# First expert weights: one load moved, one split moved to other engines, one wait dropped

## The reference, cut to what matters

```python
grp_prob = jax.nn.softmax(xr @ w_group + b_group, axis=-1)
p_grp, g_sel = lax.top_k(grp_prob, 1)
exp_logits = jnp.einsum('td,dge->tge', xr, w_router) + b_router
...
w_top, e_top = lax.top_k(jax.nn.softmax(exp_logits, axis=-1), TOP_K)
...
def expert_block(args):
    xb, e = args
    hid = jax.nn.silu(xb @ w_gate[e]) * (xb @ w_up[e])
    return hid @ w_down[e]
```

## Time and profile before

| | |
|---|---|
| median of 3 runs | 1344.77 us (1341.58 to 1347.65) |
| profiled execution | 1344.94 us, of which the span from first to last instruction is 1343.1 us |
| mean granted TensorE clock | 0.988 of full |
| busy | TensorE 96%, VectorE 67%, ScalarE 54%, GpSimd 13% |
| DMA | 273.56 MB, mean 204 GB/s; 367 to 394 GB/s in most of the experts' stage |

### The profile page before, as it was taken

How to read it: one execution, slowest core, us unless ns; L and a number is a source line. 1 busy time by engine, 2 the same in 40 slices (tenths; PEclk the granted TensorE clock), 3 DMA queues, 4 the chain that set the end, 5 groups by cost and what they waited for, 6 DMA issues and landing times. The chain is left out here.

```text
span 1343.1 us, 19059 instructions
## 1 busy us (share of the span) xinstructions
PE 1292.4 (96%) x7544; PEld 1131.8 (84%) x7544; DVE 904.8 (67%) x1060; ACT 721.5 (54%) x919; POOL 179.4 (13%) x144
## 2 busy tenths in 40 slices
PE   6999999999999999989998999999999999999997
PEld 5989998999899999967887788888888888888874
DVE  6753556355645464534237889889898989888967
ACT  6351235123512351424223778888787887887844
POOL 0020112011201120430001111111111111111100
PEclk9999999999999999999996999999999999999999
DMA  7100010000000000305514999999999999999978
GB/s 206 48 16 19 30 32 32 17 32 32 32 17 32 32 32 1 126 0 225 199 63 165 369 373 377 390 390 390 393 394 386 387 384 367 382 393 375 381 284 343
DMA packets 38047, 273.56 MB, mean 204 GB/s; under 512 B 8147, under 2 KB 8403, under 8 KB 25700
## 3 DMA queue, kind: packets, MB, share of 16 engines
q1 hardware_dynamic: 28340, 251.67, 49.4%
q0 software_dynamic: 9216, 16.80, 3.3%
q10 hardware_dynamic: 432, 4.27, 0.8%
HBM read 260.11 MB, written 29.36 MB: 216 GB/s over the span
## 5 line engine op out<-in xcount | busy, mean ns | idle before, releaser
L950 DVE TENSOR_TENSOR w_lo<-w_raw,w_hi 128x2048 fp32r<-128x2048 f32 x192 | 433.0, 2286 | 33.2 <-ACT w_hi L731 32.6
L731 ACT ACTIVATE w_hi<-w_raw 128x2048 fp32r<-128x2048 f32 x192 | 360.6, 1915 | 90.6 <-DMA w_raw<-in_w_up 59.2
L1285 PE MATMUL bank<-xn_hi,p_hi 128*128 128x364 f32 (+1 forms) x672 | 229.2, 341 | 2.1 <-DVE p_lo L1736 2.1
L1287 PE MATMUL bank<-xn_hi,p_lo 128*128 128x364 f32 (+1 forms) x672 | 216.8, 323 | 0.0
L1286 PE MATMUL bank<-xn_lo,p_hi 128*128 128x364 f32 (+1 forms) x672 | 216.6, 322 | 0.0
L585 PE MATMUL bank<-w_hi,xgT_hi 128*128 128x512 f32 x512 | 206.2, 403 | 2.9 <-DVE xgT_lo L1008 2.9
L587 PE MATMUL bank<-w_hi,xgT_lo 128*128 128x512 f32 x512 | 201.2, 393 | 0.0
L586 PE MATMUL bank<-w_lo,xgT_hi 128*128 128x512 f32 x512 | 200.6, 392 | 0.0
L1285 PEld LDWEIGHTS bank<-xn_hi,p_hi 128*128 128x128 f32 x672 | 127.8, 190 | 2.9 <-DVE p_lo L1736 2.5
L1286 PEld LDWEIGHTS bank<-xn_lo,p_hi 128*128 128x128 f32 x672 | 128.0, 190 | 0.3
L1287 PEld LDWEIGHTS bank<-xn_hi,p_lo 128*128 128x128 f32 x672 | 127.6, 190 | 0.0
(11 more groups left out here) (253 smaller groups left out, 2023.1 us busy)
## 6 DMA issues: line engine op xcount, KB each, us to landing
w_raw<-in_w_down SPq DMA_DIRECT2D x32, 2048.0 KB, 10.4
w_raw<-in_w_gate SPq DMA_DIRECT2D x31, 2048.0 KB, 11.0
w_raw<-in_w_up SPq DMA_DIRECT2D x31, 2048.0 KB, 10.0
p_raw<-in_w_tiles SPq DMA_DIRECT2D x28, 512.0 KB, 3.3
arena<-y_rows SPq DMA_DIRECT2D x8, 1024.0 KB, 14.1
arena<-in_tokens SPq DMA_DIRECT2D x10, 416.0 KB
w_out_raw<-in_w_out SPq DMA_DIRECT2D x4, 1024.0 KB, 8.8
arena<-in_tokens SPq DMA_DIRECT2D x8, 512.0 KB, 4.4
```

Of the source, the lines that this page charges most:

```text
L731: nc.scalar.activation(w_hi[m][:, half], wraw[m][:, half], ACT.Copy).then_inc(hi_done[m], 1)
L950: nc.vector.tensor_tensor(w_lo[m][:, half], wraw[m][:, half], w_hi[m][:, half].bitcast(F32), ALU.subtract).then_inc(lo_done[m], 1)
L1285: nc.tensor.matmul(out[:, 0:n], p_hi[slot][:, k, :], hi, start=(k == 0), stop=False)
L1287: m = nc.tensor.matmul(out[:, 0:n], p_lo[slot][:, k, :], hi, start=False, stop=(k == KD - 1))
```

## The change

Four edits.

1. The routing's scratch tensors move off slot 2's raw buffer: `slot1h`, `ids`, `wparts` and the weights to where `w_out_hi` lay, the rest to just behind the raw buffer.
2. With that buffer free after the last `y_low`, SyncE issues the first down load in the output stage at t = 5, right behind the store of that step's h rows; it waits for `y_hi` and `y_lo` of all tiles. It goes from its old place.
3. ScalarE splits the first gate matrix right after its last norm of the output stage, once the output products are done, ahead of the routing's exponentials. The low part moves from VectorE to GpSimd: two subtractions of 128x2048 between GpSimd's memsets and its first gather.
4. SyncE no longer waits for the first gather ahead of the second gate load; it waits for hi and lo of the first gate matrix alone.

```diff
+        zt = Zone(NF - KD * L, NF)
+        slot1h = place("slot1h", zt.at, 2 * NT, 128)
...
+        zr = Zone(zy.end - 8320 + WU, zy.end - 8320 + 7680)
...
                 sp.dma_start(h_dram[rows, :], h_sb[t % 3]).then_inc(h_stored, 16)
+                if t == 5:
+                    sp.wait_ge(y_hi_done, 5)
+                    sp.wait_ge(y_lo_done, 5)
+                    load_unit(sp, 0, 2)
...
             sp.wait_ge(x2_stored, NT * 16)
-            sp.wait_ge(gathered[0], 16)
...
             refill(1, 0, 1)
-            sp.wait_ge(gathered[1], 16)
-            sp.wait_ge(tables, 2)
-            load_unit(sp, 0, 2)
...
+            act.wait_ge(out_done, 2 * NT)
+            split(0, 0)
             act.wait_ge(r_dve, GRP_DIFF)
...
-            split(0, 0)
             act.wait_ge(h_stored, 16 * NT)
...
             ts(stab[:, 0:E], bank[0][:, E:2 * E], float(BIG), None, ALU.add)
-            split(0, 0)
...
             nc.gpsimd.memset(zero_rows, 0.0).then_inc(zero_set, 1)
+            for b in range(2):
+                half = slice(b * WU // 2, (b + 1) * WU // 2)
+                pool.wait_ge(hi_done[0], b + 1)
+                nc.gpsimd.tensor_tensor(w_lo[0][:, half], wraw[0][:, half], w_hi[0][:, half].bitcast(F32),
+                                        ALU.subtract).then_inc(lo_done[0], 1)
             pool.wait_ge(xg_zero, 2)
```

More of the change, by code:

```diff
@@ L307, in layer_kernel @@
         lo_done = [sem(f"w_lo_done{i}") for i in range(3)]
[L310 to L319, removed]
+        zt = Zone(NF - KD * L, NF)
+        slot1h = place("slot1h", zt.at, 2 * NT, 128)
+        zt.take(2 * NT, 128)
+        ids = place("ids", zt.at, 2 * NT, 2 * E)
+        zt.take(2 * NT, 2, E)
+        wparts = place("wparts", zt.at, 2 * NT, 2 * E)
+        zt.take(2 * NT, 2, E)
+        weight_hi = place("weight_hi", zt.at, 2 * NT)
+        zt.take(2 * NT)
+        weight_lo = zt.take(2 * NT)
+        zr = Zone(zy.end - 8320 + WU, zy.end - 8320 + 7680)
         ids_v, wparts_v = (v.rearrange("p a (k e) -> p a k e", k=2) for v in (ids, wparts))
```

## The result

The changed kernel takes 1351.54 us (median of 13 runs, 1348.32 to 1355.5), the kernel before 1344.77 (13 runs, 1341.58 to 1347.71). The ratio is 1.0051 with a 95% interval of 1.0039 to 1.0064: slower by 6.8 us where 7.1 were forecast. The profiled execution took 1354.84 us with a span of 1353.0, one of the longer runs. In it ScalarE's last instruction of the last norm starts 1.70 us later than before (707.67 us against 705.97). The early down load does not explain it: in the eight kernels of the experiments that start lies between 703.97 and 707.89 us, and seven of them have that load. So I count from the start of that instruction in each profile.

What follows compares the result with a forecast made beforehand. TensorE bounds the experts' stage, whose start VectorE's routing chain sets; 1344.94 + 8.8 - 1.4 - 0.3 = 1352.0 us. The range was 1344 to 1355 us, with slower at 0.50, same 0.47, faster 0.03.

Steps and rivals of the forecast that it cites:

- The block: VectorE's routing chain: two-SBUF-input operations stand until each GpSimd subtraction half ends, +8.8 us; both halves block, chance 0.75.
- no block: Rival in the routing: VectorE's tiny operations slip through beside GpSimd's subtractions; 1343.2 us, chance 0.12.
- one half that blocks: Rival in the routing: VectorE, once through, keeps ahead of GpSimd's second half; +2.7 us, 1347.6 us, chance 0.10.
- VectorE relieved: Behind the index table: taking the 4.48 us subtraction off VectorE gives 0, since the chain ahead is not shortened.
- ScalarE early: After the last norm: ScalarE's first gate split moves earlier and the exponentials do not wait; cost 0.
- The loads: Start of experts: earlier down and second gate loads let the second up load land sooner; first down product -1.4 us.
- the third rival: Start of experts: the early loads bring no gain; 1353.7 us, counted within the 0.75 for both halves blocking.
- The -0.3 us: Next four experts, 71.56 us against 70.92: part of the 0.6 us credited to lighter DMA, -0.3 us.
- The clock: TensorE's first products at half clock: a later start could shift about 2 us either way; taken as 0.

Runs made afterwards that it cites:

- low_on_vector: The changed kernel with the two low-part subtractions back on VectorE behind the index tables; 1343.37 us, ratio 0.9990.
- one_half: The changed kernel with the low part's first half on GpSimd and its second half back on VectorE; 1345.61 us, ratio 1.0001.
- fill_beside: The changed kernel with the low part back on VectorE and seven GpSimd memsets of 128x1024 in place of the subtractions; 1343.10 us, ratio 0.9983.
- eight_pieces: The changed kernel with GpSimd's low part cut into eight subtractions of 128x512 in place of two of 128x2048; 1348.92 us, ratio 1.0037.
- down_load_alone: The kernel before with the scratch tensors moved and the first down load at t = 5, nothing else; 1341.29 us, ratio 0.9983.
- split_alone: The kernel before with only ScalarE's first gate split early and its low part on GpSimd; 1351.61 us, ratio 1.0049.
- wait_back: The changed kernel with SyncE's wait for the first gather put back ahead of the second gate load; 1350.39 us, ratio 1.0044.

## Why the prediction was right

**The block.** Forecast +8.8 us at the index table, measured 23.12 - 14.56 = 8.56, by one operation in each GpSimd half as forecast. The sum is closer than its parts.

The prediction had line 898 of the kernel before held by the first half; GpSimd caught line 896 in that half, two operations ahead, and line 898 in the second, so the number of held operations was as forecast and the first of them was not. The chain's next operation (line 907, 905 before) starts 11.12 us behind the norm in place of 2.80, 8.32 us later: 0.5 less than forecast, 0.4 of it because GpSimd took 4.49 us a half in place of the estimated 4.68, the rest because the held operation ended with GpSimd's half and needed next to none of its 0.17 us behind it. The other 0.24 us came back between lines 963 and 969, 1.36 us in place of 1.13, beside TensorE's counting products at a granted clock of 0.50.

low_on_vector (8.2 us back), one_half (one operation, 4.51 us) and fill_beside (0.06 us) show that it is the cause, that it goes by instruction, and that the two-input operations are held by a GpSimd that reads SBUF and not by one that only writes. By the Trainium skill's rule ("SBUF — State Buffer", Who interferes with whom), a GpSimd instruction that only writes does not contend with a VectorE instruction that has two SBUF inputs; fill_beside agrees, with 0.17 us for lines 898 and 900. The rivals of no block and of one half that blocks both fell. One reading of the prediction was too narrow: that the price is for operations with two SBUF inputs. In eight_pieces the scalar operation of line 907, with one tensor input, was held as well.

**VectorE relieved, ScalarE early.** Both forecast at 0. The first gate product moved by 8.67 us against 8.56 for the index table, so the 4.48 us taken from VectorE behind it came back nowhere, as forecast. low_on_vector and down_load_alone have the ScalarE split early and late, and the index table at 14.57 in both.

**The loads.** Forecast -1.4 us at the first down product: the distance from the first gate product fell from 23.27 to 21.85, which is 1.42. The landing of the second up load was forecast at 7.5 us and was 7.6. The path was the forecast one too: VectorE's part of the hidden rows starts right behind its own subtractions, 20.90 us behind the first gate product in place of 22.32. But that this term belongs to the early loads is shown by down_load_alone only where there is no block. In split_alone, with the block and without the loads, the wait is gone as well: the distance is 0.75 us shorter than before, in spite of a longer stretch at half clock that cost 0.7. So in the changed kernel the term was right in size, and partly by luck: the third rival's time, 1353.7 us, was not measured, but its claim that the loads bring no gain there is not refuted. Of the two load edits the early down load is the one that matters; wait_back shows none for the other.

**The -0.3 us** for the next experts is below what the medians resolve, and the traces do not give it to the loads: the four experts from the third turn on took 71.56 us before and 70.94 in the changed kernel, but 70.93 in split_alone, without the early loads, and 71.62 in low_on_vector, with them. **The clock**, forecast at 0, cost nothing in the first gate product, where half clock lasted 4.4 us in the changed kernel as before; the 0.24 us ahead of it are named above. The sum came to 6.8 us in the medians against 7.1, so it stood on the edge of 0.5%, where the chances had put it.

## What to carry to other kernels

Before work is given to an idle GpSimd, look at what VectorE does at that very time. Here it ran a chain of small operations with two inputs in SBUF, and each GpSimd instruction that read SBUF held the chain for nearly its whole length; cutting it into eight gave back 1.3 of 8.6 us. Look for the block in the durations of VectorE's operations, not in the waits. The work that VectorE did behind the point where the next stage was decided cost nothing here, so moving it could gain nothing.

## What the runs showed of the hardware

- A blocked operation is recorded as busy: 4.44 us for 12 elements per partition, beside 0.17.
- GpSimd was not seen to be slowed by the chain that it held: 8.97 us for its two halves, where the earlier trace rows gave an estimate of 9.35, and 9.89 us for the same in eight pieces.
- `TENSOR_SCALAR` (line 907), with one tensor input in SBUF, was held as well, 1.19 us in place of 0.17 in eight_pieces, while the reductions passed at 0.17 to 0.25. Beside GpSimd's fills it took 0.23 us; whether a fill held it for that short time is open.
- The chain's stop reached TensorE's clock: after 10.27 idle us its two counting products of line 550 took 0.74 us at a granted clock of 0.50, and 0.46 us in the kernel before at 1.00.
